# The output products of an RWKV chunk loop: 64 weight columns a pass on two partition halves, or 32 on four quarters

## The chip, the cores and the metric

The kernel runs on one core of a Trainium2 chip. The metric is the device time of one execution in microseconds (us). Its engines are called TensorE (PE in the profile; its weight loads are PEld), VectorE (DVE), ScalarE (ACT), GpSimd (POOL) and SyncE (SP), which issues the loads.

## The reference

A model of two blocks over 256 tokens of width 1024, in float32. The change lies in the first block, in the state recurrence of RWKV-7 with 16 heads of 64:

```python
def step(S, inp):
    r_t, w_t, k_t, v_t, a_t, b_t = inp
    sa = jnp.einsum('bhvk,bhk->bhv', S, a_t)
    S = S * w_t[:, :, None, :] + sa[..., None] * b_t[:, :, None, :] + v_t[..., None] * k_t[:, :, None, :]
    y = jnp.einsum('bhvk,bhk->bhv', S, r_t)
    return S, y
```

Around it stand projections, a causal convolution of 31 taps with a layer norm, gates, and feed-forward layers; the second block has a Mamba-2 mixer and an attention layer. None of these is edited.

## The kernel before

The large layers are products of 128x128 weight blocks with 256 tokens (L447 to L449). Each float32 weight block is split into a high part by ScalarE (L487) and a low part by VectorE (L493), and three passes make one product.

The recurrence is computed in chunks of 32 tokens (CHUNK), eight of them (NCHUNK), in the loop at L2358. All engines run the same loop in the order in which their code is written; semaphores join them. For chunk c, TensorE does in this order:

- L2372, L2376: what the chunk takes from its own earlier tokens and from the state, into banks 4 and 5. ScalarE copies it out (L988, L989).
- L2324 (with the helper at L2184): the keys of the next chunk turned; ScalarE copies (L930, L931).
- L2286 to L2288: two (later one, at the end three) blocks of the layer "z", which only fill the time; VectorE takes them out (L1590) and splits further weights (L493). Ahead of the next step z_out at L2384 waits until VectorE has done so.
- L2387: the first part of the output, state by R, into bank 7. Sixteen heads; an even head uses partitions 0 to 63 of the state and writes partitions 0 to 63 of the bank, an odd head 64 to 127 of both. It ends with y1_done, for which VectorE's scaling of the state (L1675) waits. In the last chunk L2393 follows, a broadcast of a per-head factor.
- L2399: the inverse applied, four partition quarters, into bank 4. VectorE (L1666, L1667) and ScalarE (L1018, L1019) copy two quarters each.
- L2310: the Gram blocks of the next chunk; VectorE masks them (L1623, twice). In chunks 5 and 6 sums over the features follow (L2179).
- L2416: the change of the state, one bank; VectorE adds it (L1632), and the next chunk's L2376 waits for that.
- L2420: the second part of the output, added into bank 7 on top of L2387. Its two operands uv and g_buf lie in one half of the partitions, the lower for even chunks and the upper for odd ones (q is the parity); the output goes to both halves by head. It ends with y2_done, for which ScalarE's copy of the output (L1027) waits.

Between L1632 and the next L1590 VectorE works on taps of the convolution (L1614) in chunks 0 to 4. One matmul in plain float32 shows as two passes in the trace, each with a weight load of its own; "passes" below are these. The list quarter at L167 holds four slices of 32 partitions, side at L166 two of 64. Two other products of small blocks already write quarters: L2271, ahead of the loop, whose pairs of heads write two banks, and L2354, which turns the inverses with 128 rows by 32 columns.

Of the kernel before, what the change touches and what calls it, by code (L numbers as in the profile page):

```python
# [36 lines left out]
RWKV_HEADS, HEAD = 16, 64  # L37
CHUNK = 32
# [41 lines left out]
def build(nc, a, out):  # L80
    ctx = ExitStack()
    with ctx:
        sems = {}

        def sem(name):
            if name not in sems:
                sems[name] = ctx.enter_context(nc.semaphore(name))
            return sems[name]
# [44 lines left out]
        def slot(i):  # L133
            return pj[:, 8 * i:8 * i + 8, :]


        R, K, V, U, GATE, BK, KK, A, TMP, W, G = 0, 1, 2, 3, 4, 5, 7, 8, 9, 10, 11
# [28 lines left out]
        side = [slice(64 * q, 64 * q + 64) for q in range(2)]  # L166
        quarter = [slice(CHUNK * r, CHUNK * r + CHUNK) for r in range(4)]  # L167
        g_buf = [region[side[q], 0:1024].rearrange("p (h n) -> p h n", h=RWKV_HEADS) for q in range(2)]
        uv = [region[side[q], 1024:2048] for q in range(2)]
# [18 lines left out]
        state = flat_sub[:, 2048:2560].rearrange("p (m v) -> p m v", m=KC)  # L188
# [60 lines left out]
        pb = [ctx.enter_context(nc.psum_tensor(f"pb{i}", [P, 512], F32)) for i in range(8)]  # L249
# [1904 lines left out]
        def _(pe):  # L2154
            mm = pe.matmul
# [26 lines left out]
            def turn(o, i):  # L2182
                n = i.shape[0]
                return pe.transpose(o, i, ident[0:n, 0:n])  # L2184
# [6 lines left out]
            for k in range(KC):  # L2191
                for c in range(2):
                    ins = turn(pb[3 + k // 2][:, T * (k % 2) + P * c:T * (k % 2) + P * c + P], x_tok[:, c, P * k:P * k + P])
# [97 lines left out]
            def z_out(last):  # L2291

                pe.wait_ge(sem("evac_done"), L["z"].evac0 + BANKS + min(last, len(L["z"]) * M_PER_UNIT))


            def x_out(h):

                i, r = h // 8, h // 2 % 4
                return pb[4 + h % 2][quarter[r], 64 * i:64 * i + 64]
# [34 lines left out]
            for q in range(PE_PAIRS):  # L2334
                if q == 1:
                    z_out(Z_EARLY)
                for s in range(CONV_TAPS):
                    i = CONV_TAPS * q + s
                    pe.wait_ge(sem("tap_ready"), 2 * i + 2)
                    for c in range(2):  # L2340
                        for a in range(2):
                            ins = mm(pb[4 + 2 * q + a][side[c], s:T], diag[(2 * i + c) % NDIAG][side[a], :],
                                     slot(U)[side[a], 2 * q + c, 0:T - s], start=s == 0, stop=s == CONV_TAPS - 1, skip_group_check=True)
# [5 lines left out]
            for i in range(CHUNK // INV_GROUP):  # L2349
                for j in range(INV_GROUP):  # L2350
                    for r in range(4):

                        pick = ident[:, :].rearrange("p (y r h) -> p r y h", r=4, h=2)[:, r]
                        ins = mm(pb[4 + i][quarter[r], 32 * j:32 * j + 32], mt[:, :, INV_GROUP * i + j], pick, start=True, stop=True)  # L2354
# [3 lines left out]
            for c in range(NCHUNK):  # L2358
                t, q = slice(CHUNK * c, CHUNK * c + CHUNK), c % 2

                pe.wait_ge(sem("v_rows"), c + 1)
                pe.wait_ge(sem("g_masked"), c + 1)
                if c:
                    pe.wait_ge(sem("u_rows_v"), c)
                    pe.wait_ge(sem("u_rows_a"), c)
                if c == LN_SUM + 1:
                    pe.wait_ge(sem("ln_centred"), 1)
                if c == LN_VAR + 1:
                    pe.wait_ge(sem("ln_act"), 2)
                for h in range(RWKV_HEADS):  # L2370
                    m = h // 2
                    mm(x_out(h), g_buf[q][0:CHUNK, h, CHUNK:2 * CHUNK], uv[q][0:CHUNK, 64 * h:64 * h + 64], start=m < 4, stop=False, skip_group_check=True)  # L2372
                pe.wait_ge(sem("state_ready"), c + 1)
                for h in range(RWKV_HEADS):
                    m, rows = h // 2, side[h % 2]
                    ins = mm(x_out(h), slot(KK)[rows, m, t], state[rows, m, :], start=False, stop=m >= 4, skip_group_check=True)  # L2376
                ins.then_inc(sem("x_done"), 1)
                if c + 2 < NCHUNK:
                    chunk_keys(c + 1)
                if c:  # L2380
                    pe.wait_ge(sem("y_out"), c)
                z_blocks(Z_FIRST[c], Z_FIRST[c + 1])

                z_out((Z_FIRST[c + 1] - 1) // 2 * 2 + 1)  # L2384
                for h in range(RWKV_HEADS):
                    m, rows = h // 2, side[h % 2]
                    ins = mm(pb[7][rows, CHUNK * m:CHUNK * m + CHUNK], state[rows, m, :], slot(R)[rows, m, t],  # L2387
                             start=m == 0, stop=False, skip_group_check=True)
                ins.then_inc(sem("y1_done"), 1)
                if c + 1 == NCHUNK:  # L2390
                    for h in range(RWKV_HEADS):
                        m = h // 2
                        ins = mm(pb[m // 2][64 * (h % 2):64 * (h % 2) + 64, T * (m % 2):T * (m % 2) + T],  # L2393
                                 ident[0:RWKV_HEADS, h:h + 1].broadcast_to([RWKV_HEADS, 64]), bonus, start=True, stop=True)
                    ins.then_inc(sem("bonus_out"), 1)
                pe.wait_ge(sem("x_rows_a"), c + 1)
                for h in range(RWKV_HEADS):
                    i, r = h // 8, h // 2 % 4
                    ins = mm(pb[4][quarter[r], P * i + 64 * (h % 2):P * i + 64 * (h % 2) + 64], inverse[quarter[r], 2 * (c % 4) + c // 4, i, h % 2, :],  # L2399
                             x_buf[quarter[r], h % 2, i, :], start=True, stop=True)  # L2400
                ins.then_inc(sem("u_done"), 1)
                if c + 1 < NCHUNK:
                    chunk_products(c + 1)
                if c == LN_SUM:
                    pe.wait_ge(sem("conv_ready"), PE_TILES + 1)
                    feature_sums(pb[5][:, 0:T], slot(GATE)).then_inc(sem("ln_mean"), 1)
                if c == LN_VAR:
                    pe.wait_ge(sem("ln_act"), 1)
                    feature_sums(pb[5][:, 0:T], slot(U)).then_inc(sem("ln_var"), 1)
                pe.wait_ge(sem("u_rows_v"), c + 1)  # L2410
                pe.wait_ge(sem("u_rows_a"), c + 1)
                if c + 1 < NCHUNK:
                    pe.wait_ge(sem("bk_rows"), c + 1)
                    z_out(Z_FIRST[c + 1])
                    for h in range(RWKV_HEADS):
                        ins = mm(pb[6][64 * (h % 2):64 * (h % 2) + 64, 64 * (h // 2):64 * (h // 2) + 64],  # L2416
                                 bk_t[q][:, 64 * h:64 * h + 64], uv[q][:, 64 * h:64 * h + 64], start=True, stop=True)
                    ins.then_inc(sem("s_done"), 1)
                for h in range(RWKV_HEADS):
                    ins = mm(pb[7][64 * (h % 2):64 * (h % 2) + 64, CHUNK * (h // 2):CHUNK * (h // 2) + CHUNK],  # L2420
                             uv[q][:, 64 * h:64 * h + 64], g_buf[q][:, h, 0:CHUNK], start=False, stop=h >= 14, skip_group_check=True)
                ins.then_inc(sem("y2_done"), 1)
            z_out(len(L["z"]) * M_PER_UNIT)
            pe.wait_ge(sem("y_out"), NCHUNK)
# [39 lines left out]
            for i, src in enumerate((acs[:, 0:P], acs[:, P:T], dt[:, 0:P], dt[:, P:T], da_end)):  # L2464
                ins = turn(pb[4][:, SSD_HEADS * i:SSD_HEADS * i + SSD_HEADS], src)
# [14 lines left out]
            for c in range(2):  # L2480
                t = slice(P * c, P * c + P)
                for g in range(SSD_GROUPS):
                    ins = mm(pb[6 + c][:, P * g:P * g + P], xbc[:, 16 + g, t], xbc[:, 20 + g, t], start=True, stop=True)
                ins.then_inc(sem("cb_done"), 1)
            for g in range(SSD_GROUPS):
                ins = turn(pb[5][:, P * g:P * g + P], xbc[:, 16 + g, 0:P])
# [24 lines left out]
            for i in range(17):  # L2511
                if i >= 1:
# [9 lines left out]
                    for r in range(4):  # L2522
                        h = 4 * hq + r
                        ins = mm(pb[2 + j % 2][64 * (h % 2):64 * (h % 2) + 64, P * (r // 2):P * (r // 2) + P],
                                 xdt[:, c, 64 * h:64 * h + 64], att[j % NATT][:, r, :], start=c == 0, stop=True, skip_group_check=c == 1)
# [55 lines left out]
            for i in range(FOX_UNITS + 3):  # L2581
                if i < FOX_UNITS:
# [5 lines left out]
                    for h in range(2):  # L2588
                        m, rows = heads[h] // 2, slice(64 * (heads[h] % 2), 64 * (heads[h] % 2) + 64)
                        ins = mm(pb[i % 2][:, n * h:n * h + n], q_t[rows, m, P * qc:P * qc + P], k_t[rows, m, 0:n], start=True, stop=True)  # L2590
# [5 lines left out]
                if i % 2 == 0 and i < FOX_UNITS:  # L2596
# [4 lines left out]
                    for k in range(KC):  # L2601
                        mm(pb[5][:, 0:T], w_hi[w][:, k, :], x_hi[:, k, :], start=k == 0, stop=False)
                        mm(pb[5][:, 0:T], w_hi[w][:, k, :], x_lo[:, k, :], start=False, stop=False)
                        ins = mm(pb[5][:, 0:T], w_lo[w][:, k, :], x_hi[:, k, :], start=False, stop=k == KC - 1)
                    ins.then_inc(sem("block_done"), 1)
                if 2 <= i < FOX_UNITS + 2:
# [5 lines left out]
                    for h in range(2):  # L2612
                        for b in range(nb):
                            ins = turn(pb[2 + j % 2][:, P * (nb * h + b):P * (nb * h + b) + P], sc[s][:, h, P * b:P * b + P])
                    ins.then_inc(sem("turned"), 1)
                if i >= 3:
                    j = i - 3
                    q, r = divmod(j, O_GROUP)
# [7 lines left out]
                    for h in range(2):  # L2626
                        f = HEAD * heads[h]
                        o = HEAD * (heads[h] % (2 * O_GROUP))
                        for b in range(nb):
                            ins = mm(pb[4 + 3 * (q % 2)][:, o:o + HEAD],  # L2630
                                     pt[s][:, P * (nb * h + b):P * (nb * h + b) + P], v_tok[:, b, f:f + HEAD], start=b == 0, stop=b == nb - 1)
# [64 lines left out]
```

## Time and profile before

| | us |
|---|---|
| median of three runs | 1409.23 |
| lowest, highest | 1406.98, 1414.4 |
| the profiled execution | 1408.89 |
| its span, first to last instruction | 1407.0 |
| TensorE busy | 1339.2 (95%) |
| TensorE weight loads busy | 1275.6 (91%) |
| VectorE busy | 1003.6 (71%) |
| ScalarE busy | 772.8 (55%) |
| GpSimd busy | 104.0 (7%) |

Mean granted TensorE clock: 0.976 of full speed. The profile is of one execution. A busy share says how full an engine is over the whole span, not where it sets the pace; the chain of waits says that. The chunk loop takes some 120 us of the span. In a row of the order of time several instructions of one line are merged: "x32" are 32 passes, the first number is the start of the first, and the second runs to the end of the last, with the length of that last pass in it.

### The profile page before, as it was taken

How to read it: one execution, taken by the hardware profiler on the slowest of the kernel's cores; microseconds unless marked ns; L12 is line 12 of the kernel's file. 1: busy time of each engine (PE TensorE's matmuls, PEld its weight loads, DVE VectorE, ACT ScalarE, POOL GpSimd, SP SyncE). 2: the span in 40 equal slices, each digit the busy share in tenths (PEclk: the TensorE clock that was granted, in tenths of full speed). 3: DMA queues.
4: the chain of work that ended last, by engine and by line, in shares of the span. 5: the costliest groups of instructions: out<-in, count | busy, mean ns of one | idle time of the engine just before them, and what ended most of it. 6: DMA issues, size and time to landing. Idle time of an engine off the chain costs nothing.

```text
span 1407.0 us, 30277 instructions
## 1 busy us (share of the span) xinstructions
PE 1339.2 (95%) x12494; PEld 1275.6 (91%) x12494; DVE 1003.6 (71%) x1658; ACT 772.8 (55%) x1348; POOL 104.0 (7%) x130
## 2 busy tenths in 40 slices
PE   5999999999999999999998899999999998999998
PEld 5998968888999999989896799999999887999986
DVE  4769898975977665477798967787565655888754
ACT  4595396547656443445568645444455455644553
POOL 2000100000001111000101001221000100011100
PEclk8999999988999999999999899999999999999999
DMA  7633620211554555645573165555665521555462
GB/s 223 204 125 118 192 83 10 85 61 47 168 183 146 180 180 160 202 151 182 178 222 96 45 212 178 180 179 166 195 185 169 188 66 55 193 183 190 152 215 71
DMA packets 199539, 211.65 MB, mean 150 GB/s; under 512 B 8924, under 2 KB 190956, under 8 KB 199292
## 3 DMA queue, kind: packets, MB, share of 16 engines
q1 hardware_dynamic: 197180, 201.46, 44.8%
q0 software_dynamic: 2144, 8.46, 2.1%
q8 instruction: 90, 1.47, 0.4%
q14 instruction: 29, 0.24, 0.1%
q10 hardware_dynamic: 96, 0.02, 0.0%
HBM read 208.28 MB, written 1.64 MB: 149 GB/s over the span
## 4 chain that ended last, share of the span: by engine, by line
PE 79%; DVE 11%; ACT 5%; DMA 2%; SPq 2%; issue 1%; POOL 0%; DVEq 0%; ACTq 0%
PE pb L447 20%; PE pb L449 20%; PE pb L448 20%; DVE w_lo L493 2%; ACT pj L951 2%; PE pb L2664 1%; PE pb L2665 1%; PE pb L2663 1%; PE pb L2173 1%; PE pb L2184 1%; SPq L599 1%; PE pb L2590 1%; DVE pj L1614 1%; DMA raw<-in_ffn_w_down_dram 1%; PE pb L2286 1%
## 5 line engine op out<-in xcount | busy, mean ns | idle before, releaser
L487 ACT ACTIVATE w_hi<-raw 128x1024 fp32r<-128x1024 f32 (+2 forms) x384 | 396.4, 1041 | 317.3 <-PE pb L449 247.5
L493 DVE TENSOR_TENSOR w_lo<-raw,w_hi 128x1024 fp32r<-128x1024 f32 (+2 forms) x384 | 467.3, 1220 | 136.7 <-ACT w_hi L487 135.8
L447 PE MATMUL pb<-x_hi,w_hi 128*128 128x256 f32 x1920 | 547.2, 285 | 7.8 <-DVE w_lo L493 3.8
L448 PE MATMUL pb<-x_lo,w_hi 128*128 128x256 f32 x1920 | 544.1, 283 | 0.0
L449 PE MATMUL pb<-x_hi,w_lo 128*128 128x256 f32 x1920 | 544.0, 283 | 0.0
L447 PEld LDWEIGHTS pb<-x_hi,w_hi 128*128 128x128 f32 x1920 | 369.5, 192 | 11.3 <-DVE w_lo L493 8.7
L448 PEld LDWEIGHTS pb<-x_lo,w_hi 128*128 128x128 f32 x1920 | 369.4, 192 | 0.2
L449 PEld LDWEIGHTS pb<-x_hi,w_lo 128*128 128x128 f32 x1920 | 369.3, 192 | 0.0
L732 POOL TENSOR_TENSOR sub<-sub,rstd 128x256 f32<-128x256 f32 x66 | 72.0, 1106 | 717.9 <-ACT sub L1101 717.9
L447 PE MATMUL pb<-act_hi,w_hi 128*128 128x256 f32 x392 | 111.1, 284 | 3.2 <-DVE w_lo L493 3.2
L449 PE MATMUL pb<-act_hi,w_lo 128*128 128x256 f32 x392 | 110.9, 283 | 0.0
L448 PE MATMUL pb<-act_lo,w_hi 128*128 128x256 f32 x352 | 99.6, 283 | 0.0
L1101 ACT ACTIVATE sub<-sub 128x256 f32<-128x256 f32 x66 | 26.5, 415 | 101.1 <-DVE sub L1817 84.4
L447 PEld LDWEIGHTS pb<-act_hi,w_hi 128*128 128x128 f32 x392 | 75.2, 192 | 3.6 <-DVE w_lo L493 3.6
L449 PEld LDWEIGHTS pb<-act_hi,w_lo 128*128 128x128 f32 x392 | 75.3, 192 | 0.0
L448 PEld LDWEIGHTS pb<-act_lo,w_hi 128*128 128x128 f32 x352 | 67.6, 192 | 0.0
L1788 DVE TENSOR_TENSOR sub<-pb,rstd 128x256 f32<-128x256 f32 x66 | 27.7, 423 | 45.7 <-PE pb L449 43.3
L1794 DVE TENSOR_TENSOR sub<-pb,sub 128x256 f32<-128x256 f32 x66 | 27.7, 420 | 39.7 <-PE pb L449 22.2
L1108 ACT ACTIVATE act_hi<-sub 128x256 f32 (+1 forms) x66 | 27.3, 416 | 44.7 <-DVE sub L1794 44.7
L1392 DVE TENSOR_TENSOR pj<-pb,rstd 128x256 f32<-128x256 f32 x72 | 30.2, 421 | 28.8 <-PE pb L449 27.5
L1614 DVE SCALAR_TENSOR_TENSOR pj<-pj,par 128x255 f32<-128x255 f32 (+29 forms) x120 | 48.3, 465 | 0.9
L2184 PE MATMUL pb<-ident,pj 128*128 128x128 f32 (+1 forms) x211 | 36.3, 315 | 11.4 <-DMA pj<-in_x_dram 6.0
(344 smaller groups left out, 2222.2 us busy)
## 6 DMA issues: line engine op xcount, KB each, us to landing
raw<-in_ffn_w_up_dram SPq DMA_DIRECT2D x55, 1024.0 KB, 5.1
raw<-in_w_in_dram SPq DMA_DIRECT2D x28, 1024.0 KB, 5.1
raw<-in_ssd_w_in_dram SPq DMA_DIRECT2D x20, 1024.0 KB, 5.4
raw<-in_ffn_w_down_dram SPq DMA_DIRECT2D x16, 1024.0 KB, 5.3
raw<-in_fox_w_in_dram SPq DMA_DIRECT2D x16, 1024.0 KB, 5.7
raw<-in_ffn_w_down_dram SPq DMA_DIRECT2D x16, 896.0 KB, 5.1
raw<-in_ffn_w_gate_dram SPq DMA_DIRECT2D x11, 1024.0 KB, 5.3
raw<-in_ssd_w_out_dram SPq DMA_DIRECT2D x8, 1024.0 KB, 5.2
```

The source lines that it names most:

```text
L447: pe.matmul(o, w_hi[m][:, k, :], hi[:, k0 + k, :], start=first and k == 0, stop=False)
L448: pe.matmul(o, w_hi[m][:, k, :], lo[:, k0 + k, :], start=False, stop=False)
L449: mm = pe.matmul(o, w_lo[m][:, k, :], hi[:, k0 + k, :], start=False, stop=final and k == nk - 1)
L487: act.activation(piece(ly, u, w_hi[m], nk, m), raw_piece(ly, u, s, nk, m), ACT.Copy).then_inc(sem("w_hi_ready"), 1)
L493: dve.tensor_tensor(piece(ly, u, w_lo[m], nk, m), raw_piece(ly, u, s, nk, m), piece(ly, u, w_hi[m], nk, m).bitcast(F32), ALU.subtract).the ...
L732: pool.tensor_tensor(s_tile[m], s_tile[m], rstd[:, :], ALU.mult).then_inc(sem("glu_silu"), 1)
L951: act.activation(diag[n % NDIAG], ident2[:, :], ACT.Copy, scale=par_col("conv_dw_pe", 2 * (CONV_TAPS * q + CONV_TAPS - 1 - s) + c)).then_i ...
L1392: tt(o, pb[m][:, 0:T], rstd[:, :], ALU.mult).then_inc(sem("evac_done"), 1)
L1614: go(stt(o[:, s:T], c[:, 0:T - s], w, o[:, s:T], ALU.mult, ALU.add))
L1788: tt(g_tile[m], pb[m][:, 0:T], rstd[:, :], ALU.mult).then_inc(sem("evac_done"), 1)
L1794: tt(a_tile[m - 2], pb[m][:, 0:T], s_tile[m - 2], ALU.mult).then_inc(sem("evac_done"), 1)
L2184: return pe.transpose(o, i, ident[0:n, 0:n])
```

## The change

In both output products a head's 64 weight columns are taken in two passes over 32, so that the output is written quarter by quarter. For each head v counts the two halves of its columns, and the quarter written is 2 (h mod 2) + v. In L2387 the order of the heads changes too: m, then v, then the even and the odd head. In L2420 the two halves of a head follow each other. What is computed, the bank, the start and stop marks and the semaphores stay. The Gram products (L2310) and the others are untouched.

```diff
-                for h in range(RWKV_HEADS):
-                    m, rows = h // 2, side[h % 2]
-                    ins = mm(pb[7][rows, CHUNK * m:CHUNK * m + CHUNK], state[rows, m, :], slot(R)[rows, m, t],
-                             start=m == 0, stop=False, skip_group_check=True)
+                for y in range(2 * RWKV_HEADS):
+                    m, v, h = y // 4, y // 2 % 2, y % 2
+                    ins = mm(pb[7][quarter[2 * h + v], CHUNK * m:CHUNK * m + CHUNK], state[side[h], m, CHUNK * v:CHUNK * v + CHUNK],
+                             slot(R)[side[h], m, t], start=m == 0, stop=False, skip_group_check=True)
                 ins.then_inc(sem("y1_done"), 1)
...
                 for h in range(RWKV_HEADS):
-                    ins = mm(pb[7][64 * (h % 2):64 * (h % 2) + 64, CHUNK * (h // 2):CHUNK * (h // 2) + CHUNK],
-                             uv[q][:, 64 * h:64 * h + 64], g_buf[q][:, h, 0:CHUNK], start=False, stop=h >= 14, skip_group_check=True)
+                    for v in range(2):
+                        ins = mm(pb[7][quarter[2 * (h % 2) + v], CHUNK * (h // 2):CHUNK * (h // 2) + CHUNK],
+                                 uv[q][:, 64 * h + CHUNK * v:64 * h + CHUNK * v + CHUNK], g_buf[q][:, h, 0:CHUNK],
+                                 start=False, stop=h >= 14, skip_group_check=True)
                 ins.then_inc(sem("y2_done"), 1)
```

## Rows read from the trace of the kernel before

**Rows 1.** The page: shares of the chain by engine, and a weight product's idle.

```profile
span 1407.0 us, 30277 instructions
...
PE 79%; DVE 11%; ACT 5%; DMA 2%; SPq 2%; issue 1%; POOL 0%; DVEq 0%; ACTq 0%
...
L447 PE MATMUL pb<-x_hi,w_hi 128*128 128x256 f32 x1920 | 547.2, 285 | 7.8 <-DVE w_lo L493 3.8
```

**Rows 2.** By source line: passes, ns of one (min/median/max), first and last start, tile.

```profile
L2387 PE MATMUL pb<-pj,sub x256: 219/219/313, 229.5 to 330.4; 64*64 64x32 f32 x128
L2271 PE MATMUL pb<-pj x256: 186/193/215, 128.6 to 135.3; 64*32 64x32 f32 x128
```

**Rows 3.** Order of time, chunk 0: start us, us, engine, line, tile, passes [idle before].

```profile
229.52 1.12 PE L2387 MATMUL pb<-pj,sub 64*64 64x32 f32 x32
230.57 0.69 PE L2399 MATMUL pb<-pj 32*32 32x64 f32 x32
231.19 1.15 PE L2310 MATMUL pb<-pj 64*64 64x64 f32 x32
231.34 0.41 DVE L1666 COPY pj<-pb 32x256 f32<-32x256 f32 x1 [1.28 <-PE pb L2399]
232.25 1.15 PE L2416 MATMUL pb<-pj,sub 64*64 64x64 f32 x32
233.24 1.07 PE L2420 MATMUL pb<-pj 64*64 64x32 f32 x32
234.38 0.56 PEld L2372 LDWEIGHTS pb<-pj 32*32 32x32 f32 x32 [0.19 <-issue]
234.41 0.69 PE L2372 MATMUL pb<-pj 32*32 32x64 f32 x32
235.22 0.30 PEld L2376 LDWEIGHTS pb<-sub,pj 64*32 64x32 f32 x32 [0.28 <-DVE sub L1632]
235.22 0.46 PE L2376 MATMUL pb<-sub,pj 64*32 64x64 f32 x32
```

**Rows 4.** The chain that ended last, through the loop: start us, us, what.

```profile
234.48 0.70 DVE sub L1632
...
262.37 1.52 DVE pj L1614 x4
...
282.47 1.92 PE pb L2387 x32
...
289.01 1.65 PE pb L2420 x29
...
300.69 3.65 PE pb L2179 x16
...
318.84 0.91 PE pb L2420 x32
```

**Rows 5.** Order of time, TensorE: bursts outside the loop.

```profile
128.55 1.29 PE L2271 MATMUL pb<-pj 64*32 64x32 f32 x128
...
135.09 0.36 PE L2271 MATMUL pb<-pj 64*32 64x32 f32 x31 [1.23 <-issue]
...
197.73 13.82 PE L2342 MATMUL pb<-pj 64*64 64x256 f32 x248
...
213.90 6.02 PE L2354 MATMUL pb<-ident,sub 128*32 128x32 f32 x256
```

**Rows 6.** Order of time: L1666 in chunks 1, 3, 4; L2420 in chunk 7.

```profile
244.17 0.42 DVE L1666 COPY pj<-pb 32x256 f32<-32x256 f32 x1 [0.15 <-PE pb L2399]
...
271.82 0.42 DVE L1666 COPY pj<-pb 32x256 f32<-32x256 f32 x1
...
285.51 0.41 DVE L1666 COPY pj<-pb 32x256 f32<-32x256 f32 x1 [0.83 <-PE pb L2399]
...
336.68 1.92 PE L2420 MATMUL pb<-pj 64*64 64x32 f32 x32 [1.02 <-DVE pj L1667]
```

**Rows 7.** Chunks 4 and 5: us, PE busy (passes), clock, DMA share, GB/s.

```profile
275.30:306.60 31.30, 28.79 (x532) 0.78 0.14 45
```

## Prediction: step by step

> **What bounds the kernel now.** The page comes first: the chain that ended last lies on TensorE for 79% of the span [rows 1]. Time taken from TensorE where that chain runs is therefore time gained, unless another engine is just behind. The profiled execution took 1408.89 us around a span of 1407.0 us; the median of the runs is 1409.23, so 0.34 us above it. The sum below is made against 1408.89 and the 0.34 is added at the end.
>
> Both edited parts lie in the chunk loop, between about 221 and 340 us. Second view: the lines by source. L2387 issues 256 passes, 32 in each of eight chunks, which is two passes for each of the 16 matmuls [rows 2], and L2420 as many. Third view, the order of time in chunk 0 [rows 3]: L2387 shows 1.12 us for 32 passes. One pass lasts 219 ns from start to end [rows 2], and I take 0.21 to 0.22 for the last pass of the other full-clock bursts too, so the starts are (1.12 - 0.22) / 31 = 29 ns apart. L2420 is the same at (1.07 - 0.22) / 31 = 27 ns. L2310 moves 64 elements a pass where L2387 moves 32, and it has the same 30 ns. So these passes are not paced by what is streamed; the 64 weight columns, or a fixed turn of a tile, pace them. The passes that already have 32 weight columns and 64 moved elements are 15.4 ns apart (L2372, L2399: (0.69 - 0.21) / 31), and 7.7 ns apart where both row halves and four quarters take part (L2376: (0.46 - 0.22) / 31).
>
> Fourth view, the chain through the loop [rows 4]. In chunk 0 it goes L2387, L2399, then to VectorE (L1666, L1667, L1675, L1623, L1632) and back to L2376. L2420 is not in it: it lies beside the VectorE work, with TensorE idle 0.19 us before L2372 and 0.28 us before L2376 [rows 3]. So L2387 is on the path in chunk 0 and L2420 is not. Where each is in the later chunks is read from the same view below.
>
> **Part one, L2387.** Sixteen matmuls (32 passes) become 32 matmuls (64 passes), each with 32 weight columns and 32 moved elements. Two tiles were in turn (row half 0 with columns 0 to 63, row half 1 with columns 64 to 127). Now four are: two row halves by two quarters each. The row with exactly this shape is the first burst of L2271, 64 rows by 32 columns with 32 moved elements: 128 passes in 1.29 us, so (1.29 - 0.19) / 127 = 8.6 ns apart [rows 5]. It has eight tiles in turn, not four, and its row halves write two banks, not one. That is the optimistic end. The other end is 15.4 ns, L2399, which has four tiles in turn and whose four row quarters write one bank [rows 3]. At 8.6 ns L2387 takes 63 x 8.6 + 193 = 0.73 us instead of 1.12, a saving of 0.39. At 15.4 it takes 1.19, a loss of 0.07. I take 8.6. The two 15.4 ns rows and L2376 move 64 elements, and all have their number of tiles times the spacing at about 62 ns; L2342, which moves up to 256, needs 13.82 us for 248 passes, 55 ns a pass or about 220 ns for its four tiles [rows 5]. The turn of a tile thus grows with the moved elements, and L2387 had 58 ns with 32 of them only because it loaded 64 columns. With both at 32 nothing in the trace holds the turn at 60 ns.
>
> At the lower clock L2387 of chunk 4 shows 1.92 us [rows 4], 52 ns a pass, 1.8 times as much. New: 63 x 8.6 x 1.8 + 0.29 = 1.27 us, a saving of 0.65.
>
> What of it counts, chunk by chunk. Chunk 0: VectorE idled 1.28 us before L1666, so all 0.39 counts. Chunks 1 and 2: L1666 starts after an idle of only 0.15 us [rows 6], because VectorE's L493 ends just ahead; I leave 0.03 of it for the hand-over, so 0.12 each counts, together 0.24. Chunk 3: L1666 starts with no idle at all, and the chain lies on VectorE's conv taps L1614 before it and again between it and chunk 4 [rows 4, 6]: zero. Chunk 4: idle 0.83 [rows 6], so 0.65 counts. Chunks 5, 6: the chain runs on over TensorE through the sums of L2179 [rows 4] (one row of two), 0.39 each. Chunk 7: it runs L2387, L2393, L2399, so 0.39. Sum: 0.39 + 0.24 + 0 + 0.65 + 3 x 0.39 = 2.45 us.
>
> **Part two, L2420.** The same doubling, but all tiles lie in one row half (that of the chunk's parity) and only the four quarters are in turn. The trace has no such row. Nearest from below: L2271 at 8.6 ns. Then L2372, one row quarter by four column quarters, at 15.4 ns with 64 moved elements [rows 3]. From above: L2354, 128 rows by four column quarters with 32 moved elements, 256 passes in 6.02 us, (6.02 - 0.22) / 255 = 22.7 ns [rows 5]; both its operands are strided, which those of L2420 are not. I take 8.6, because L2420 now (27 ns, one row half) and L2310 (30 ns, both row halves) show that two tiles beside each other in one row half overlap as well as two in different halves. New: 0.73 us against 1.07, a saving of 0.34. One thing is added. Between L2416 and L2420 the tile shape now changes from 64 by 64 to 64 by 32. Without a change L2420's first start is 0.06 us after L2416's last; across the change from L2387 to L2399 it is 0.15 [rows 3]. So 0.09 is lost and 0.25 is left.
>
> The Trainium skill, TensorEngine Tiling (Array Packing), section Key Properties, says that a switch of the tiling mode drains the engine. These rows agree and price it at 0.09 us more than no switch.
>
> What counts: in chunks 0 to 3 and 5 L2420 is beside VectorE's work [rows 3, 4], so nothing. There it could also be longer by 0.47 us, the two idles of rows 3, before it costs anything. In chunk 4 it is on the chain at the lower clock, where I take the 1.92 us of chunk 7: 0.65 less twice 0.09, 0.47. In chunk 6 it is on the chain: 0.25. In chunk 7 it follows a wait of 1.02 us for VectorE, so its switch is hidden, and it runs at the lower clock: 0.65 [rows 4, 6]. Sum 1.37 us.
>
> **What follows from both.** No semaphore, wait, DMA or copy changes; y1_done and y2_done hang on the last pass as before. VectorE's L1675 waits for y1_done and ScalarE's L1027 for y2_done, and both come earlier. Behind the loop the weight products run with 7.8 us of idle in 1920 passes of L447 [rows 1], so TensorE keeps what it is given. 512 more passes have to be supplied. In the long L2271 row supply fails once: after 97 passes it idled 1.23 us [rows 5], with nothing in the profile to wait for. In the chunk loop no row of 32 passes shows that, and I cost it at nothing.
>
> Total 2.45 + 1.37 = 3.8 us: 1408.89 - 3.8 = 1405.1, with 0.34 added **1405.4**.
>
> **The rivals.** (A) The turn of a tile is about 60 ns whatever its width (15.4 ns with four tiles). For it: 55 to 62 ns in six lines of rows 3, and L2271 with eight tiles at 69. Against: L2342's 220 ns, and L2271's 69 may be a limit of issue. L2387 loses 0.07 in six chunks, 0.4 in all; L2420 loses 0.1 and the switch 0.09 where it is exposed, some 0.4. The time is 1409.2 + 0.8 = 1410.0. (B) Only L2420 fails, since its quarters share a row half. At 15.4 ns it gives -2.45 + 0.4: 1407.2. At 22.7 ns it grows by 0.57 + 0.09, of which 0.19 shows in each of chunks 0 to 2, 0.34 in chunk 5, 0.66 in chunk 6, and at the lower clock 1.13 and 0.95 in chunks 4 and 7, 3.7 in all: 1410.4. (C) The slower side: passes in 32-column tiles that share a bank or a row half don't overlap at all, and keep their 29 ns. L2387 is 63 x 29 + 220 = 2.05 us, 0.93 more in six chunks, 0.4 in chunk 3 and 1.7 in chunk 4: 7.7. L2420 pays 0.56 in each of chunks 0 to 2, 0.7, 0.9, and twice 1.7: 6.7. The time is 1423.6. It decides from 14.6 ns a pass on, where 64 passes equal the old 32. Against it stand L2399 and L2372, one bank and one row quarter, both at 15.4.
>
> Two statements of the Trainium skill would lead to C. TensorEngine Tiling (Array Packing), section Gotcha 1: PSUM Pressure, says that different row tiles cannot access the same PSUM bank at once, which would hit L2387. TensorE: Matmul & The Clock Gate, section The mechanism, says that weight loads overlap running matmuls only if the row group differs, which would hit L2420. By either the sum would be that of C for its line. The rows of L2399 and L2372 speak against both.
>
> (D) Supply of instructions: one stall of 1.23 us in each chunk would be 9.8 us, 1415.2; in half of them 1410.3. (E) The granted clock. Over chunks 4 and 5 its mean is 0.78 [rows 7], full speed (2.4 GHz) for part of them and the half level (1.2 GHz) for the rest. Of 31.3 us, 22% is 6.9 us of missing clock; VectorE's share of the chain does not slow with it, so I put the price at 5.6 us, an estimate. Shifted starts can add or remove such a stretch: 1411 or 1399.8.
>
> **How the numbers follow.** Forecast 0.42, A 0.25, B 0.15, D 0.07, E 0.06 (half each way), C 0.05. The range from 1402 to 1411.5 holds the forecast, A, B and the milder half of D. Half a per cent, 7 us, is about what a measurement of this kernel can tell from no change, and every main case lies within it. Faster by more needs E: 0.04. Slower by more is C and the worst of D: 0.07. Same: 0.89.
>
> **What would show it.** L2387 and L2420 with 64 passes each a chunk and 0.73 us at full clock: right. 1.15 to 1.2 us: A. L2387 short and L2420 long: B. About 2 us: C. A row split in two with an idle marked issue: D. If L2420 shortens in chunk 0, the idle before L2372 and L2376 should grow from 0.47 us and L2376 should start where VectorE lets it. In chunks 1 and 2 L1666 should follow its neighbour with no idle, and chunk 3 should keep its length. The forecast is wrong if the loop shortens by less than 2 us with short bursts: then VectorE takes back more than I gave it.

## The result and the profile after

The changed kernel takes 1415.68 us, the median of 17 runs (1409.96 to 1420.6), against 1411.55 us for the kernel before in as many runs beside it. The ratio is 1.003, with a 95% interval of 1.0017 to 1.0043: slower by 2.4 to 6.1 us, where 3.8 us less had been forecast. The forecast of 1405.4 us stood on the three first runs of the kernel before (1409.23 us); the 17 runs beside the changed one put it 2.3 us higher, and that part of the distance has nothing to do with the change. The profiled execution took 1413.63 us around a span of 1411.6 us.

First the page of the kernel after: span, engines, chain, the instruction queue and a weight product. The lines answer to [rows 1].

```profile
span 1411.6 us, 31301 instructions
...
PE 1337.0 (95%) x13006; PEld 1272.4 (90%) x13006; DVE 1003.9 (71%) x1658; ACT 772.8 (55%) x1348; POOL 104.0 (7%) x130
...
PE 77%; DVE 11%; ACT 5%; DMA 2%; issue 2%; SPq 2%; POOL 0%; DVEq 0%; ACTq 0%
...
q8 instruction: 94, 1.54, 0.5%
...
L447 PE MATMUL pb<-x_hi,w_hi 128*128 128x256 f32 x1920 | 548.8, 286 | 7.6 <-DVE w_lo L493 3.9
```

1024 instructions are new, as the diff says: 512 passes and 512 weight loads. Two lines move. In the chain "issue", time in which an engine waited for nothing that the profile shows, went from 1% to 2%, and TensorE from 79% to 77%. And q8, an instruction queue, has 94 packets where the kernel before has 90, so it is the one that brings TensorE its instructions. The 1024 new instructions are four packets, so a packet holds 256, and 1.54 MB over 94 packets is 16 KB each.

Second view, the lines by source (passes, ns of one as min/median/max), then the order of time in chunk 0, as in [rows 3].

```profile
L2387 PE MATMUL pb<-pj,sub x512: 192/193/215, 232.9 to 337.8; 64*32 64x32 f32 x171
L2421 PE MATMUL pb<-pj x512: 187/193/258, 236.3 to 344.6; 64*32 64x32 f32 x171
```

```profile
232.87 0.76 PE L2387 MATMUL pb<-pj,sub 64*32 64x32 f32 x64
233.56 0.69 PE L2399 MATMUL pb<-pj 32*32 32x64 f32 x32
234.33 0.41 DVE L1666 COPY pj<-pb 32x256 f32<-32x256 f32 x1 [0.92 <-PE pb L2399]
235.24 1.15 PE L2416 MATMUL pb<-pj,sub 64*64 64x64 f32 x32
236.32 0.76 PE L2421 MATMUL pb<-pj 64*32 64x32 f32 x64
237.37 0.80 PEld L2372 LDWEIGHTS pb<-pj 32*32 32x32 f32 x32 [0.41 <-issue]
238.26 0.45 PE L2376 MATMUL pb<-sub,pj 64*32 64x64 f32 x32
```

Both bursts are short. L2387 took 0.76 us instead of 1.12, and L2421 (L2420 before) 0.76 instead of 1.07. L1666 starts 1.46 us after L2387 where it was 1.82. VectorE's idle before it fell from 1.28 to 0.92 us. The stretch from L2387 to L2376 shrank from 5.70 to 5.39 us. So the direct gain is there in chunk 0. The idles before L2372 and L2376 should have grown from 0.47 us together. That before L2372 grew from 0.19 to 0.41 us, but that before L2376 is gone, since L2372 itself took 0.93 us where it was 0.69.

Where it went is seen in the order of time two chunks on, TensorE's rows at the seam of chunks 1 and 2 and of chunks 4 and 5. In between lies VectorE's idle before L1590.

```profile
249.08 0.76 PE L2421 MATMUL pb<-pj 64*32 64x32 f32 x64
250.16 0.69 PE L2372 MATMUL pb<-pj 32*32 32x64 f32 x32 [0.32 <-DVEq L1626]
250.96 0.35 PE L2376 MATMUL pb<-sub,pj 64*32 64x64 f32 x17
253.78 0.47 PE L2376 MATMUL pb<-sub,pj 64*32 64x64 f32 x15 [2.47 <-issue]
...
260.65 0.42 DVE L1590 TENSOR_TENSOR pj<-pb,rstd 128x256 f32<-128x256 f32 x1 [3.31 <-PE pb L2288]
...
294.03 1.08 PE L2421 MATMUL pb<-pj 64*32 64x32 f32 x64
...
296.06 0.46 PE L2376 MATMUL pb<-sub,pj 64*32 64x64 f32 x15
298.43 0.52 PE L2376 MATMUL pb<-sub,pj 64*32 64x64 f32 x17 [1.90 <-issue]
```

In two chunks L2376's 32 passes are cut in two. The second part comes 2.47 and 1.90 us later and waits for no semaphore. That is 4.4 us, and the chain of waits runs through the first: "250.96 0.35 PE pb L2376", then 2.47 us of issue. The kernel before shows no such row in its loop.

The DMA view tells what the engine waited for. I counted all of TensorE's instructions in the trace from the start: weight loads, passes, and the waits and register instructions between them (loads and passes alone don't come out even). The weight load that resumes in [rows 5] inside L2271 is number 2241; those above are 6082 and 8130. They differ by 15 and by 8 times 256, to within one. The same count over the whole program in all 14 profiles of this case finds 35 idles of over 0.15 us marked issue ahead of a pass, and every one leaves the same remainder by 256, to within one. The stalls therefore lie at borders of packets. The two windows are the stretch of the load that L632 issued at 247.08, up to TensorE's stop, and the 1.3 us behind it (packets, MB, share of the 16 engines).

```profile
247.08 0.37 SPq L632 DMA_DIRECT2D raw<-in_w_in_dram  x1
...
DMA packets 957, 0.98 MB, mean 362 GB/s; under 512 B 3, under 2 KB 957, under 8 KB 957
...
q1 hardware_dynamic: 957, 0.98, 103.2%
...
q1 hardware_dynamic: 454, 0.04, 27.4%
q8 instruction: 1, 0.02, 5.1%
```

TensorE crosses a border at 248.5 us. Only then is the packet after next wanted, and 1 MB of weights is just starting on all 16 engines (248.1 to 251.7). In the first window no q8 packet moves; the packet moves from 251.38 to 252.44, as the load ends. TensorE, which has used up its 256 instructions by 251.3, goes on at 253.78. In chunk 4 it is the same: border at 292.94, load from 292.2 to 296.2, packet at 295.73, on again at 298.43. The edit is what made this late, in two ways. It moved the borders: in the kernel before the border of the same number falls at 248.2, near the end of its load (245.1 to 249.25), and its packet starts 1.2 us later. And it made the instructions go faster: the 256 between these borders are 28 of L2416, 128 of L2421, 64 of L2372, 34 of L2376 and two waits, gone in 2.8 us.

The granted clock is the second part. It is at its half level (1.2 GHz) for 34.4 us of the loop after and for 23 us before, the loop being 123.2 us and 117.4 us long. The windows of the whole loop (us, busy time with count of TensorE, its weight loads, VectorE, ScalarE, GpSimd, then clock, DMA share, GB/s), before and after:

```profile
222.30:339.70 117.40, 112.08 (x2165) 102.76 (x2155) 88.92 (x171) 63.90 (x142) 0.00 (x0) 0.90 0.18 57
```

```profile
222.30:345.50 123.20, 112.05 (x2697) 101.43 (x2697) 88.82 (x172) 63.57 (x142) 0.00 (x0) 0.86 0.17 54
```

One of the stretches after begins inside the first stall (252.8, 6.8 us). Another begins at 222.0, ahead of any edited instruction, so part of the 11 us is variation between runs.

### The profile page after: what moved, and what is told of

The parts are those of the page before. It is cut to its first block, busy times and chain, and to the rows that moved or that the text cites. A ratio compares the mean times of both kernels' runs of the same rounds, so it can differ in the third digit from the quotient of the medians.

```text
span 1411.6 us, 31301 instructions
## 1 busy us (share of the span) xinstructions
PE 1337.0 (95%) x13006; PEld 1272.4 (90%) x13006; DVE 1003.9 (71%) x1658; ACT 772.8 (55%) x1348; POOL 104.0 (7%) x130
## 3 DMA queue, kind: packets, MB, share of 16 engines
q8 instruction: 94, 1.54, 0.5%
## 4 chain that ended last, share of the span: by engine, by line
PE 77%; DVE 11%; ACT 5%; DMA 2%; issue 2%; SPq 2%; POOL 0%; DVEq 0%; ACTq 0%
PE pb L447 20%; PE pb L449 19%; PE pb L448 19%; DVE w_lo L493 2%; ACT pj L951 2%; PE pb L2665 1%; PE pb L2667 1%; PE pb L2666 1%; PE pb L2184 1%; PE pb L2173 1%; SPq L599 1%; PE pb L2592 1%; DMA raw<-in_ffn_w_down_dram 1%; DVE pj L1614 1%; PE pb L2286 1%
```

## The experiments

Theory one, supply: the bursts gain what was forecast, and a packet of instructions that is wanted just as a weight load begins costs more than that. Its rival: the gain is lost because of what the edited passes do themselves (the bank or row half they share, the switch of tile, one of the two parts), or because of the clock alone.

**A shift that did nothing: e1 and e2.** Empty instructions at the head of TensorE's program should have moved the borders, in the changed kernel away from the loads, in the kernel before onto one.

```diff
     pe.wait_ge(sem("const_ready"), 1)
+    for _ in range(176):   # e2, on the kernel before: 96
+        pe.nop()
```

> The changed kernel with 176 empty instructions ahead of everything on TensorE, where it waits for the first load anyway. They move the places where TensorE crosses from one block of 256 instructions to the next. Theory (supply): the changed kernel loses its gain because TensorE uses up a block in under 3 us inside a 1 MB weight load, so the fetch of the next block, which starts only when the load ends, comes 2.4 and 1.9 us late (chunks 1 and 4). Moved by 176, no crossing falls so in chunks 1 to 4, and one in chunk 6 may wait up to 0.7 us. Expected: both stalls inside L2376 gone, the chunk loop 4 to 6 us shorter than in the changed kernel, time 2 to 4 us below the kernel before. Rival (the narrow passes themselves lower the granted clock, or the gain was never there): the time stays 3 to 5 us above the kernel before, and the clock in the loop stays low without stalls.

> The kernel before with 96 empty instructions ahead of everything on TensorE; its wide passes are kept. Theory (supply): moved by 96, a crossing falls into L2416 of chunk 3 just after the weight load begins and the next one some 3.5 us later, so TensorE stalls about 2.3 us in chunk 3, near L2376 of chunk 4, with no change of the passes; the loop is 2 to 3 us longer, more if the clock falls behind it. Rival (the stalls belong to the narrow passes): no stall, time within 1 us of the kernel before.

Measured: e1 1.0028 (1.0012 to 1.0043), e2 1.0009 (0.9994 to 1.0023). But e1 has 31301 instructions, as many as the changed kernel, and e2 30277, as many as the one before: the empty instructions are not in the compiled program. Both are repeats. As such they are worth something. e1 shows the two stalls again, at the same instructions 6082 and 8130 (lines are two higher):

```profile
251.80 0.46 PE L2378 MATMUL pb<-sub,pj 64*32 64x64 f32 x15 [2.45 <-issue]
...
296.93 0.35 PE L2378 MATMUL pb<-sub,pj 64*32 64x64 f32 x17 [2.85 <-issue]
```

e2, the kernel before once more, has none in the loop. The stalls belong to the program, not to a run.

**Each part alone: e3, e4.** e3 has only the hunk of L2387, e4 only that of L2420.

```diff
+                for y in range(2 * RWKV_HEADS):            # e3: this hunk alone
...
+                    for v in range(2):                     # e4: this hunk alone
```

> Only L2387 is changed. Theory (supply): the crossings lie at other places (chunk 1 in L2387 and L2420, chunk 4 in L2387 and L2416), and no block is used up inside a load, so no stall; L2387 at 0.76 us a chunk in place of 1.12; gain 2 to 2.5 us against the kernel before. Rival (narrow passes lower the clock or the gain is taken back by VectorE): no gain or a loss, without a stall.

> Only L2420 is changed. Theory (supply): direct gain 0.3 us in chunk 6 and up to 0.6 in each of chunks 4 and 7, but a crossing falls into L2416 of chunk 2 at the start of its weight load, the next about 2 us later in L2376 of chunk 3: a stall of 2 to 2.9 us there; net 1 to 3 us slower than the kernel before. Rival (the loss comes from L2420 itself, whose quarters share a row half): L2421 longer than 1.07 us, loss spread over all chunks, no single stall.

Measured: e3 0.9989 (0.9973 to 1.0004), e4 1.0015 (1.0002 to 1.0029). The order of time of e3, chunk 0, and of e4, the seam of chunks 2 and 3:

```profile
229.64 0.76 PE L2387 MATMUL pb<-pj,sub 64*32 64x32 f32 x64
...
232.99 1.07 PE L2420 MATMUL pb<-pj 64*64 64x32 f32 x32
```

```profile
261.09 0.76 PE L2421 MATMUL pb<-pj 64*32 64x32 f32 x64
...
262.97 0.41 PE L2376 MATMUL pb<-sub,pj 64*32 64x64 f32 x21
265.78 0.45 PE L2376 MATMUL pb<-sub,pj 64*32 64x64 f32 x11 [2.39 <-issue]
```

Each part shortens its burst to 0.76 us. e3 has no stall in the loop. e4 has one of 2.39 us, in the burst that the count had given. e4 alone does not tell the two theories apart, since its bad part is also the part with the shared row half; the next group does.

**The same changed loop with the borders moved: e5, e6, e11.** Tiny products of the identity ahead of everything, whose results are overwritten, move the borders by four instructions each: 44, 32 and 49 of them.

```diff
     pe.wait_ge(sem("const_ready"), 1)
+    for i in range(44):   # e6: 32, e11: 49
+        mm(pb[7][quarter[i % 4], 0:CHUNK], ident[quarter[i % 4], 0:CHUNK], ident[quarter[i % 4], 0:CHUNK], start=True, stop=True)
```

> The changed kernel with 44 tiny products of the identity ahead of everything on TensorE, where it waits for the first load anyway: 176 rows of loads and passes. They move the crossings between blocks of 256 instructions by 176. Theory (supply): both stalls in L2376 (before chunk 2 and chunk 5) are gone, at most 0.7 us is lost near chunk 6, the loop is 4 to 6 us shorter than in the changed kernel and the time is 1 to 4 us below the kernel before. Rival (the narrow passes lower the clock by themselves): no stall either, but the time stays 3 us or more above the kernel before.

> The same with 32 tiny products, 128 rows. Theory (supply): the two stalls go and one comes, where a crossing falls into L2416 of chunk 3 just behind the start of its weight load: about 2.9 us inside the L2376 that follows (chunk 4's), after 25 of its 32 passes. Time between the kernel before and the changed one, 0 to 3 us above before. Rival: the stalls stay where the changed kernel has them.

> The changed kernel with 49 tiny products ahead, 196 rows. Theory (supply): counted from the start of L2416 the first crossing of a dense stretch falls at row 14 in chunk 0 (no weight load there, stall of about 1.2 us), 94 in chunk 1 (about 0.3 us), outside in chunks 2 to 4; together 1 to 2 us instead of 4.4 and more. Time from 2 us below to 0.5 us above the kernel before, clock as in it. Rival (narrow passes cost by themselves): 3 us or more above.

Measured: e5 1.0016 (0.9999 to 1.0032), e6 0.9993 (0.9975 to 1.0011), e11 0.9984 (0.9964 to 1.0004). The idles marked issue in their loops, e5 first, then e6, then e11:

```profile
236.49 0.33 PE L2378 MATMUL pb<-sub,pj 64*32 64x64 f32 x11 [1.10 <-issue]
...
278.73 0.41 PE L2374 MATMUL pb<-pj 32*32 32x64 f32 x6 [1.86 <-issue]
...
318.47 0.31 PE L2378 MATMUL pb<-sub,pj 64*32 64x64 f32 x6 [0.62 <-issue]
```

```profile
282.29 0.46 PE L2378 MATMUL pb<-sub,pj 64*32 64x64 f32 x14 [2.45 <-issue]
```

```profile
235.96 0.64 PE L2378 MATMUL pb<-sub,pj 64*32 64x64 f32 x21 [0.24 <-issue]
...
253.07 0.28 PE L2288 MATMUL pb<-x_hi,w_hi 128*128 128x256 f32 x1 [0.94 <-issue]
```

The two old stalls are gone in each. e5 is a miss: it got three others, 3.6 us together, where 0.7 at most had been expected, and no gain. At the first of them no weight load runs: its packet started at 234.24, 1.2 us behind the border at 233.07, and the 256 instructions were gone in 2.3 us. e6 has the one stall expected, 2.45 us instead of 2.9 and after 18 passes of the burst rather than 25. e11 kept both its stalls as short as expected, 1.2 us together. The loop is the same code in all three and in the changed kernel, with the same edited passes. With 4.4 to 5.6 us of stall (the changed kernel three times over) the ratio is 1.002 to 1.003, with 3.6 it is 1.0016, with 2.45 it is 0.9993, with 1.2 it is 0.9984. Neighbours in this row overlap within their intervals, but those of e6 and e11 lie wholly below that of the changed kernel. No rival about the passes themselves can do that.

**The kernel before with its borders moved: e7, e12.** The same filler, 24 and 56 products, with every pass of the loop as wide as before.

```diff
     pe.wait_ge(sem("const_ready"), 1)
+    for i in range(56):   # e7: 24
+        mm(pb[7][quarter[i % 4], 0:CHUNK], ident[quarter[i % 4], 0:CHUNK], ident[quarter[i % 4], 0:CHUNK], start=True, stop=True)
```

> The kernel before, wide passes kept, with 24 tiny products ahead, 96 rows. Theory (supply): a stall of about 2.3 us appears at the end of chunk 3 or the start of chunk 4, though nothing in the loop was edited; time 2 to 4 us above the kernel before. Rival (stalls belong to the narrow passes): none, and the time within 1 us of before.

> The kernel before with 56 tiny products ahead, 224 rows; all passes wide. Theory (supply): a crossing falls into L2416 of chunk 1 at the start of its weight load: a stall of up to 2.8 us in chunk 1 or at the start of chunk 2; the time 1.5 to 4 us above the kernel before and the clock 0.001 lower. Rival (only narrow passes bring stalls and the lower clock): no stall of over 0.5 us, time and clock those of before.

Measured: e7 1.0007 (0.9994 to 1.0019). It has 0.88 and 0.71 us of stall where 2.3 in one had been expected: a miss in size, and no verdict. e12: 1.003 (1.0016 to 1.0044), 1415.58 us. Its seam of chunks 1 and 2 on TensorE, then the DMA windows up to the stop (249.3 to 252.9) and behind it (252.9 to 253.4):

```profile
250.51 1.07 PE L2422 MATMUL pb<-pj 64*64 64x32 f32 x32
251.69 0.69 PE L2374 MATMUL pb<-pj 32*32 32x64 f32 x32
252.49 0.46 PE L2378 MATMUL pb<-sub,pj 64*32 64x64 f32 x32
252.88 0.30 PE L2184 MATMUL pb<-ident,pj 128*64 128x128 f32 x1
255.51 1.70 PE L2184 MATMUL pb<-ident,pj 128*64 128x128 f32 x7 [2.33 <-issue]
```

```profile
q1 hardware_dynamic: 1156, 1.04, 95.9%
...
q1 hardware_dynamic: 199, 0.02, 30.4%
q8 instruction: 1, 0.02, 13.9%
```

L2422 is the old wide burst, 32 passes in 1.07 us. No edited pass is in this kernel, and it is as slow as the changed one. A single border at the start of a weight load was enough, because the next 256 instructions were gone in 3.3 us (borders at 249.59 and 252.88). The border alone isn't: in e9 one falls at 286.5, as a load starts, and its packet starts only at 289.34, but the next 256 instructions, blocks of z among them, last until 292.2, and there is no stall. The stall in e12 is 2.33 us of some 4.2 us lost; the rest is not seen as one wait. The filler itself is not the cause: e11 has nearly as many products and is among the fastest.

**The load taken away: e8.** The changed kernel with the borders as compiled, but the weight loads of the layers z and conv_out cut to their first eighth. The rest of those weights is left as it was in the buffer, so part of the product is not what the reference wants, and the time is that of the same instructions with less traffic.

```diff
+    if ly.name in ("z", "conv_out"):
+        dst, src = dst[:, 0:1, :], src[:, 0:1, :]
```

> The changed kernel with the weight loads of the layers z and conv_out cut to their first eighth (so these two layers compute with stale weights). The instructions of TensorE and the crossings are as in the changed kernel. Theory (supply: the fetch of a block waits behind the 1 MB load): the fetches start within 1 us of their crossings, and the stalls of 2.5 and 1.9 us shrink to under 0.7 us; the loop 4 us or more shorter than in the changed kernel. Rival (a block is simply used up faster than any fetch can come, load or no load): the stalls stay above 1.5 us.

Measured: 0.9961 (0.9946 to 0.9977), 1404.15 us. TensorE at the two old places, then the DMA window 244.4 to 246.6 that belongs to the first:

```profile
246.76 0.35 PE L2378 MATMUL pb<-sub,pj 64*32 64x64 f32 x17
247.45 0.46 PE L2378 MATMUL pb<-sub,pj 64*32 64x64 f32 x15 [0.34 <-issue]
...
288.44 0.35 PE L2378 MATMUL pb<-sub,pj 64*32 64x64 f32 x17 [0.55 <-issue]
```

```profile
q1 hardware_dynamic: 232, 0.02, 7.1%
q8 instruction: 1, 0.02, 2.6%
```

The bursts are still cut after 17 passes and at the same borders, but for 0.34 and 0.55 us instead of 2.47 and 1.90. With the engines free the packet starts 0.7 us behind the border (244.32 to 245.00), where it was 2.85. So the border decides where, and the load how long. That the whole gain of this run comes from there is not shown: with less traffic other waits can shrink too.

**Repeats: e9 and e10.** e9 is e3 again, e10 the changed kernel again, both unedited.

```diff
+                for y in range(2 * RWKV_HEADS):            # e9: this hunk alone
```

> Only L2387 changed, once more, for a tighter interval: it is the version that the earlier runs point to. Theory (supply): no stall in the loop, 1.7 to 2.5 us below the kernel before. Rival: within 0.5 us of it.

> The changed kernel once more, beside the others of this call. Both stalls in L2376, together 4 to 5.5 us; 3.5 to 4.5 us above the kernel before; mean clock about 0.002 below it.

Measured: e9 0.9975 (0.9963 to 0.9986), 1407.93 us, with no stall in the loop; e10 1.0021 (1.0006 to 1.0036), with stalls of 2.73 and 2.85 us at the same two places. Part one alone is faster than both kernels: by 3.5 us in e9 and by 1.6 us in e3, whose interval still takes in no change.

## Why the prediction was wrong

**Part one, L2387: right in its burst, not settled in what of it counts.** 0.73 us a burst was forecast and 0.76 measured, in the changed kernel and in e3. The chunk 0 test held (L1666 earlier by 0.36 us of the 0.39), and in chunk 1 L1666 follows its neighbour with no idle:

```profile
247.08 0.42 DVE L1666 COPY pj<-pb 32x256 f32<-32x256 f32 x1
...
278.33 0.42 DVE L1666 COPY pj<-pb 32x256 f32<-32x256 f32 x1
```

The second row is chunk 3, where it had no idle before and has none now, as forecast. Counted were 2.45 us. The two ratios of part one alone, 0.9989 and 0.9975, average to 2.5 us less, but part of that is a better clock (below).

**Part two, L2420: right in its mechanism, its size not settled.** The burst takes 0.76 us where 0.73 was forecast (chunks 0, 1 and 3), with all its tiles in one row half. At the half level it took 1.08 us (294.03), where the prediction's factor of 1.8 gave 1.27. The switch after L2416 still shows: L2421 starts 1.08 us after it, L2420 0.99. The 1.37 us counted can't be read from e4, since its stall of 2.39 us is larger.

**Rivals A, B, C: out.** A asked for 1.15 to 1.2 us a burst, B for a short L2387 and a long L2420, C for about 2 us. Both are 0.76. With that both statements behind C fall: 64 passes from two row halves into one bank took 0.76 us, (0.76 - 0.19) / 63 = 9 ns apart, where the Trainium skill, TensorEngine Tiling (Array Packing), section Gotcha 1: PSUM Pressure, says that different row tiles can't use a bank at once. And passes of one row half were as close in L2421, each with its weight load, where the Trainium skill, TensorE: Matmul & The Clock Gate, section The mechanism, lets weight loads overlap only if the row group differs (the same section also names a background weight buffer, which no run here shows). The trace agrees with neither statement as read in C.

**The step that failed** is the supply of instructions in "What follows from both": "In the chunk loop no row of 32 passes shows that, and I cost it at nothing." It measured 4.4 us in the profile of the changed kernel, 5.3 in e1 and 5.6 in e10, more than the whole gain. The row for it was on record, the 1.23 us in [rows 5], and it stood in rival D at 0.07. Two things were wrong with how it was used. It was taken as a price for each chunk, where it comes at a border every 256 instructions, and only where the packet is late and the 256 instructions before the next border are gone too soon. And the loop of before was taken as proof of no cost. It was only a case in which no border met the start of a load: e12 has the same loop and loses 2.33 us at one. From these traces one can estimate a stall: the wait from border to packet, plus some 2.4 us, less the time in which the 256 instructions are used up. In chunk 1 that is 2.85 + 2.4 - 2.8 = 2.45 us, where 2.47 was measured. D's figure, 1415.2 us, is close to the median of 1415.68 by luck, since D had eight stalls of 1.23 us and the chip two of 1.9 to 2.85, with the clock behind them.

**The clock, rival E**, was priced by itself, apart from D. In the runs it goes with the stalls for the most part, which doesn't show that they cause it. Its mean over all runs is 0.9739 in the changed kernel (0.9753 and 0.9745 in e1 and e10), 0.9763 to 0.9771 in the kernel before beside the experiments but 0.9755 in e2, which is the same program, and 0.9781 and 0.9790 in e3 and e9. One can put the account together: the direct gain as forecast, the stalls of the profile, and the missing clock at 0.8 us each us, which is the price that E had (5.6 of 6.9 us) and is close to what the loops of the changed kernel and e1 show: with the stalls taken off, 118.8 us with 34.4 us at the half level against 113.0 us with 19.9 us, so 5.8 us for 7.3 us of missing clock. For a difference of 0.001 in mean clock that is 1.1 us over the whole time.

| kernel | direct | stalls | clock | sum | measured |
|---|---|---|---|---|---|
| changed | -3.8 | 4.4 | 3.3 | 3.9 | 4.2 |
| e1 (the same) | -3.8 | 5.3 | 2.0 | 3.5 | 4.0 |
| e10 (the same) | -3.8 | 5.6 | 2.0 | 3.8 | 3.0 |
| e5 | -3.8 | 3.6 | 1.1 | 0.9 | 2.3 |
| e6 | -3.8 | 2.5 | 0.3 | -1.0 | -1.0 |
| e11 | -3.8 | 1.2 | -0.7 | -3.3 | -2.3 |
| e8 | -3.8 | 0.9 | -1.7 | -4.6 | -5.5 |
| e4 (part two) | -1.4 | 2.4 | 0.9 | 1.9 | 2.1 |
| e3 (part one) | -2.5 | 0 | -1.1 | -3.6 | -1.6 |
| e9 (part one) | -2.5 | 0 | -3.0 | -5.5 | -3.5 |
| e12 (before) | 0 | 2.3 | 1.4 | 3.7 | 4.2 |
| e7 (before) | 0 | 1.6 | -0.2 | 1.4 | 1.0 |
| e2 (before) | 0 | 0 | 1.8 | 1.8 | 1.3 |

(us against the kernel before; measured is the ratio less one, times 1411; each interval is some 2 us to either side; the stalls are those in the loop of the one profiled execution, the clock the mean of all runs. The stall inside L2271, ahead of the loop, was 1.23 us before and 0.27 to 1.84 us in the others, and e5 has one more of 0.82 us behind it; they are not in the column.) All but the two of part one are within 1.4 us. Those two are 2.0 us under what was measured, so either its direct gain is smaller than 2.45 us or part of it comes back as a better clock and is counted twice.

The price of the clock can be had from the runs too. Within one kernel slower runs have a lower mean clock. A straight line through time against clock, with one slope for the 262 runs whose clock is on record and a level for each kernel or repeat, falls by 0.82 us for 0.001, less than the 1.1 above. At the same clock the changed kernel is 1.9 us above the kernel before (e1 2.7, e10 1.5), e12 3.1, e4 1.3, e5 1.0 and e7 0.4 above, while e6 is 1.7, e11 1.8, e3 1.0, e9 1.2 and e8 5.0 below, each to about 1 us. (The level of the kernel before is that of the 105 runs beside the experiments; e2, the same program, stands 0.1 below it.) So the clock alone, as a rival, is out: it does not make up the difference. But of the 2.45 us counted for part one only about 1.1 is there at the same clock. How much the shorter bursts gain by themselves stays open.

**What stays open beside it.** That stalls pull the clock down was not shown. Kernels with more stall have the lower mean for the most part, and a half-level stretch begins inside the first stall, but the kernel before has such stretches without a stall, and no run moved the clock alone. Nor can I say when a packet is late without a load: between a border and the start of its packet there were mostly 0 to 1.4 us and in a few places more. The expectations of e5 and e7 had no term for that.

## What to carry to other kernels

Splitting passes into smaller tiles shortens a burst, but doubles the instructions that it uses up. Count instructions (waits too) between borders of 256 and set the time in which they are used against the 2.2 to 2.8 us that the next packet needed here from its start, plus its wait behind a large load that has just begun. A kernel without stalls of this kind may be so by its present count alone, so a cost of nothing in the trace before is no evidence for one after, and any edit that adds or takes away TensorE instructions moves every border behind it. Here the part with the larger gain, L2387 alone, is the version to keep (1407.93 us), and its borders should be looked at again after the next edit.

## What the runs showed of the hardware

- TensorE gets its instructions in packets of 256 (16 KB) by DMA: four more packets for 1024 more instructions. All 35 stalls of this kind in the 14 profiles lie at borders of 256.
- The packet after next is fetched once a border is crossed: its transfer starts 0 to 1.4 us later in most places without a load (245.55 to 245.58 in chunk 1 of the changed kernel, 233.07 to 234.24 in e5). Where TensorE had to wait for it, it went on 2.2 to 2.8 us after the start of the transfer (251.38 to 253.78 in the changed kernel). With 0.9 to 1 MB of weights just begun on the same engines (about 360 GB/s), the packet waited for the end of the load: 2.9 us from border to start in chunk 1, 2.8 us in chunk 4.
- With the loads cut to an eighth the same borders cost 0.34 and 0.55 us. A packet as late as 2.8 us cost nothing where the 256 instructions lasted 5.7 us (e9, 286.5 to 292.2).
- Small float32 tiles of 64 rows by 32 columns with 32 moved elements start 9 ns apart at full clock (64 passes in 0.76 us), in two row halves that share a bank (L2387) as in one row half (L2421).
